# A fused two-block kernel: another order of ScalarE's work at the start, a merge kept in PSUM, two later waits, one weight chunk split on VectorE

## The chip, the cores and the metric

The kernel runs on one core of one Trainium2 chip. The metric is the device time of one execution in microseconds (us). A core has five engines that run side by side, each working through its own queue in order: TensorE (PE, matrix products), VectorE (DVE), ScalarE (ACT), GpSimd (POOL) and SyncE (SP, which here issues the DMA transfers). They wait for each other on semaphores.

## What is computed

Two residual blocks on a sequence of 256 tokens of width 1024, in float32. The first has a modulation from a conditioning vector (`ada_w`), an input projection `w_in`, a Fourier mix, a bidirectional gated scan over a context and the sequence, a merge of two branches and a convolutional feed-forward part. The second has a projection `w_in_2`, banded attention, a short convolution, a pool, `w_out_2`, and an MLP. Cut to what the change touches:

```python
# first block
hx = modulate(rmsnorm(x, norm1_g), mx[:, :, 0], mx[:, :, 1])   # sequence
hc = modulate(rmsnorm(ctx, norm1_g), mc[0], mc[1])             # context
ux = hx @ w_in;  uc = hc @ w_in
y_a = fourier_mix(ux[..., fnet]) @ w_a
y_b = y_hgrn @ w_b                                             # gated with silu(u[..., g])
merged = sigmoid(ux[..., ga]) * y_a + sigmoid(ux[..., gb]) * y_b
x = x + mx[:, :, 2] * (merged @ w_out)
# second block
out = einsum('bnhqk,bnkhd->bnqhd', softmax(scores), v)         # attention outputs
x = x + concat(y_attn, y_conv, y_pool) @ w_out_2
h2 = rms_norm(x, norm2_g)
x = x + square(relu(h2 @ w_mlp1)) @ w_mlp2
```

## The kernel before

Activations are held transposed, as tiles of 128 features by 256 tokens. Each float32 operand is split into a high part in the format `fp32r` and a low part, and every product is made of three matmuls: high weights by high activations, high by low, low by high (`mm3`, lines 1434 to 1436).

**Weights.** All weights come in chunks of 128 x 2048 (1 MB), in the order of `chunk_plan`: 20 chunks of `w_in` with 16 of `ada_hi` between them, `w_a`, `w_b` (2 each), `w_out` (4), 22 of `ffn_up` with 11 of `ffn_down`, 10 of `w_in_2`, 4 of `w_out_2`, 16 of `w_mlp1` with 16 of `w_mlp2`. SP loads a chunk into one of four `raw` buffers as soon as the low part of the chunk four places before has been made (`load`, line 400). ACT copies `raw` to `whi` (`high`, line 487; for the first seven chunks in two halves, `first_high` and `high_half`, line 490). The low part `wlo` = `raw` - `whi` is made by POOL for the chunks marked `by_pool` (line 77; lines 463 and 469, in pieces of 512 columns), and by DVE for the rest (`low`, line 864). The chunks by POOL are all those ahead of `w_mlp1`, and chunks 0 to 3 of `w_mlp1`. There are three `whi` and three `wlo` buffers. `turn` numbers the split chunks; `high(q)` makes all up to q. In the MLP's loop, DVE calls `low` for two chunks ahead, then makes relu, square and low part of the activation (lines 1394 to 1404).

**Product banks.** Products go to three PSUM banks in rotation. `product_tables` lists which semaphore says that a bank has been emptied; a group waits for the one three groups before. In `w_in` chunk 6 to 9 an instruction takes sequence and context together (512 columns). Chunks 2 and 3 are emptied by ACT to `FU`, 4 and 5 through Silu to `SG` (the semaphore `fu_sg`, `project_evict`, line 587).

**The beginning on ACT** is a queue written out by hand (lines 562 to 629). `shifts` and `scales` finish the modulation, `input_high(1, ks)` makes the high part of the context's input tiles after DVE's `input_mul` (line 926), with DVE's `input_low` (line 931) behind it. Two copies to `CP` (line 629) give DVE the row for its dot products with `ada_hi`. ACT loads a table of functions when it goes from Sqrt to Silu or Sigmoid.

**The merge.** For each of the four pieces of `w_b` (24 matmuls each) DVE multiplies the product by `GB` (line 1134), adds it to `GA` (line 1137), ACT makes the high part `MGh` (line 709), DVE the low part `MGl` (line 1139). `w_out` chunk 0 needs them in order of tiles.

**Attention outputs and column sums.** ACT writes the values `VV` after `w_in_2` 8 and 9 (line 815); TensorE makes the outputs in two halves (`tp`, lines 1854 to 1856). After `w_out_2`, TensorE sums the squares `SQ3` by columns (`square_columns`, line 1698), the first two tiles of it after DVE has added others to them (line 1164), the last two in `finish_norm`, in the middle of `w_mlp1` 0.

Of the kernel before, what the change touches and what calls it, by code (L numbers as in the profile page):

```python
# [7 lines left out]
F32 = mybir.dt.float32  # L8
F32R = mybir.dt.float32r
U8 = mybir.dt.uint8  # L10
ALU = mybir.AluOpType
ACT = mybir.ActivationFunctionType
# [58 lines left out]
def weight_tables():  # L71

    plan = chunk_plan()
    place = {(name, i): n for n, (name, i, _) in enumerate(plan)}
    split = [(name, i) for name, i, _ in plan if name != "ada_hi"]
    turn = {key: q for q, key in enumerate(split)}
    by_pool = [name not in ("w_mlp1", "w_mlp2") or name == "w_mlp1" and i < 4 for name, i in split]
    hi_at, lo_at, pool_at, dve_at = [], [], 0, 0
    for q in range(len(split)):
        hi_at.append(q + 1 + min(q + 1, FINE))  # L80
        if by_pool[q]:
            pool_at += 4 if q < FINE else 1
            lo_at.append(("lo_pool", pool_at))
        else:
            dve_at += 1
            lo_at.append(("lo_dve", dve_at))
    return plan, place, split, turn, by_pool, hi_at, lo_at


def product_tables(split):  # L90

    ends, groups, claimed, emptied = {}, 0, {}, []
    for name, i in split:
        n = {"w_a": 2, "w_b": 2}.get(name, 1)
        if name == "w_in" and 6 <= i < 12 or (name, i) in (("w_out", 3), ("w_out_2", 3)):
            n = 2
        if (name, i) in (("ffn_down", 10), ("w_mlp2", 15)):
            n = 4
        groups += n
        ends[name, i] = groups  # L100
        if name == "w_in":
            e = ([("q_done", i + 1)] if i < 2 else [("fu_sg", i - 1)] if i < 6 else
                 [("one_minus", 2 * i - 11), ("one_minus", 2 * i - 10)] if i < 10 else
                 [("v_done", 2 * i - 19), ("v_done", 2 * i - 18)] if i < 12 else
                 [("ga_done", i - 11)] if i < 16 else [("gb_done", i - 15)])
        elif name in ("w_a", "w_b"):
            e = [(f"gate_{name[2]}", 2 * i + 1), (f"gate_{name[2]}", 2 * i + 2)]
        elif name in ("w_out", "w_out_2"):
            x = "x1" if name == "w_out" else "x3"
            e = [(x, 2 * i + 2)] if i < 3 else [(x, 7), (x, 8)]  # L110
        elif name == "ffn_up":
            e = [("conv", 16 * i + 16)]
        elif name == "w_in_2":
            e = [("proj", i + 1)] if i < 8 else [("val_2", 2 * i - 14)]
        elif name == "w_mlp1":
            e = [("relu", i + 1)]
        else:
            e = []
        claimed[name, i] = len(emptied)
        emptied += e  # L120
    return ends, claimed, emptied
# [49 lines left out]
def build(nc, io):  # L171
    s = {n: nc.alloc_semaphore(n) for n in SEMS}
# [64 lines left out]
    def product(name, i, j=0):  # L237
        return bank[(claimed[name, i] + j + 1) % 3]

    def flat(ap):  # L240
        return ap.rearrange("p a b -> p (a b)")
# [230 lines left out]
    def scalar(e):  # L472
# [112 lines left out]
        def project_evict(name, i, out, func, sem):  # L585
            e.wait_ge(s["gemm"], ends[name, i])
            e.activation(out, product(name, i)[:, :], func).then_inc(s[sem], 1)

        def merge_keys(li):
            h = LEVELS[li]  # L590
            if li == 0:
                e.wait_ge(s["one_minus"], 8)
                e.wait_ge(s["diag"], 2)
            else:
                e.wait_ge(s["lev"], 2 * li)
                e.wait_ge(s["kf"], li)
            e.activation(halves(flat(KM[:, :, :]), h).rearrange("p b two z -> p two b z"), key_halves(h),
                         ACT.Copy).then_inc(s["k_merged"], 1)
# [10 lines left out]
        warm(ACT.Sqrt)  # L609
        e.wait_ge(s["sq_in"], 6)  # L610
        e.activation(RC[:, 2:4], RC[:, 2:4], ACT.Sqrt, bias=eps[:, 0:1], scale=1.0 / D).then_inc(s["rms_in"], 1)
        project_evict("w_in", 2, flat(FU[:, 0:2, :]), ACT.Copy, "fu_sg")
        first_high(5, 0)
        first_high(5, 1)
        shifts(1, 2, 14)
        shifts(1, 3, 16)
        scales(1, 0, 18)
        scales(1, 1, 20)
        input_high(1, range(0, 2))
        project_evict("w_in", 3, flat(FU[:, 2:4, :]), ACT.Copy, "fu_sg")  # L620
        input_high(1, range(2, 4))
        first_high(6, 0)
        scales(1, 2, 22)
        input_high(1, (4, 5))
        first_high(6, 1)
        scales(1, 3, 24)
        input_high(1, (6, 7))
        for n in range(2):
            e.activation(CP[:, n * 512:n * 512 + 512], CB[:, n * 512:n * 512 + 512], ACT.Copy).then_inc(s["cx_row"], 1)
        for i in range(4, 20):  # L630
            high(i + 2)
            if i == 18:
                for d in range(2):
# [4 lines left out]
            if i == 19:  # L638
                e.wait_ge(s["yf_lo"], 2)
                for hp in range(2):  # L640
# [3 lines left out]
                    e.wait_ge(s["on_done"], hp + 1)  # L644
                    e.activation(SQo[:, 2 * hp:2 * hp + 2, :], ON[:, 2 * hp:2 * hp + 2, :],
                                 ACT.Square).then_inc(s["on_sq"], 1)
            if i < 6:
                e.wait_ge(s["rms_in"], 2)
                project_evict("w_in", i, flat(SG[:, 2 * (i - 4):2 * (i - 4) + 2, :]), ACT.Silu, "fu_sg")
            elif i < 10:  # L650
                for j in range(2):
                    b = product("w_in", i, j)[:, :]
                    e.wait_ge(s["gemm"], starts["w_in", i] + j + 1)
# [51 lines left out]
        for i in range(2):  # L705
            high(turn["w_b", i] + 2)
            for n in (2 * i, 2 * i + 1):
                e.wait_ge(s["merged"], n + 1)
                e.activation(MGh[:, 2 * n:2 * n + 2, :], GA[:, 2 * n:2 * n + 2, :], ACT.Copy).then_inc(s["mg_hi"], 1)

        warm(ACT.Sqrt)
        for i in range(4):
# [144 lines left out]
    def vector(e):  # L857
# [273 lines left out]
        for n in range(4):  # L1131
            f = slice(2 * n, 2 * n + 2)
            e.wait_ge(s["gemm"], starts["w_b", 0] + n + 1)
            e.tensor_tensor(flat(GB[:, f, :]), product("w_b", n // 2, n % 2)[:, :], flat(GB[:, f, :]), ALU.mult).then_inc(s["gate_b"], 1)
            e.wait_ge(s["gate_b"], n + 1)
            e.wait_ge(s["gate_a"], n + 1)
            e.tensor_tensor(GA[:, f, :], GA[:, f, :], GB[:, f, :], ALU.add).then_inc(s["merged"], 1)  # L1137
            e.wait_ge(s["mg_hi"], n + 1)
            e.tensor_tensor(MGl[:, f, :], GA[:, f, :], MGh[:, f, :].bitcast(F32), ALU.subtract).then_inc(s["mg_lo"], 1)

        e.wait_ge(s["side"], 24)
        e.tensor_tensor(MODX[:, 0:24], MODX[:, 0:24], v("ada_b", 16, 24), ALU.add).then_inc(s["mods"], 1)
# [269 lines left out]
    def tensor(e):  # L1412
# [293 lines left out]
        bs = misc("col1")  # L1706
# [135 lines left out]
            if i == 8:  # L1842
                turn_probabilities(1)
        e.wait_ge(s["pt_done"], 6)
        e.wait_ge(s["val_2"], 4)
        for tp in range(2):
            b = misc(f"av{tp}")
            for j in range(2):
                for par in range(2):
# [17 lines left out]
        for i in range(3):  # L1867
            pair("w_out_2", i, MXh, MXl, order2, ready=mixed if i == 0 else None)
        pair("w_out_2", 3, MXh, MXl, order2, apart=True)
        e.wait_ge(s["sq3_sum"], 2)  # L1870
        square_columns(bs, SQ3, 0, 2)

        def h4_ready(k):
            e.wait_ge(s["h4_hi"], k + 1)
            e.wait_ge(s["h4_lo"], k + 1)

        def finish_norm():
            for j in range(2):
                e.wait_ge(s["sq3"], 4 + j)
                m = square_columns(bs, SQ3, 6 + j, 1)  # L1880
            m.then_inc(s["col_x"], 1)
# [139 lines left out]
```

## Time and profile before

| | us |
|---|---|
| median of 3 runs | 745.47 |
| the runs | 749.41, 745.47, 740.64 |
| the profiled execution | 743.66 |
| its span, first to last instruction | 741.8 |

All times in the rows are us from the start of this span unless marked ns. "PE" rows are matmuls, "L1434" is line 1434 of the kernel, "[... <-X]" says how long the engine was idle ahead of the instruction and what ended it. "issue" is idle time for which the profile shows no releaser. "PEclk" is the clock that TensorE was granted, as a share of full speed.

### The profile page before, as it was taken

To read this page: it belongs to the slowest core of one execution; us is meant where nothing else is said; L and a number is where in the kernel's file an instruction comes from. 1 tells how busy PE (TensorE), PEld (TensorE's weight loads), DVE (VectorE), ACT (ScalarE), POOL (GpSimd) and SP (SyncE) were. 2 spreads that over 40 slices of the span, in tenths; PEclk is the share of its full clock that TensorE was granted. 3 is DMA by queue.
4 is the path that set the end of the run, shared out by engine and by line. 5 is a ranking of instruction groups with operands and counts; after the bars stand their busy time and mean duration, and the time that the engine had idled before them with its cause. 6 is when DMAs were issued, how large, how long until landed. Compare 5 with 4: busy or idle time off the path is not lost.

```text
span 741.8 us, 14168 instructions
## 1 busy us (share of the span) xinstructions
PE 718.3 (97%) x5844; PEld 695.2 (94%) x5844; DVE 496.1 (67%) x905; ACT 360.5 (49%) x459; POOL 402.3 (54%) x223
## 2 busy tenths in 40 slices
PE   6899999999999989999999999999999899999998
PEld 3798789999999989999999999999999899999997
DVE  3877797669536569877777774558865465566663
ACT  6688134245444456555555546445554344334331
POOL 0776544556549957888878887766795400000000
PEclk9999999999999989999999999999999999999999
DMA  9994888337534537455555554433435545655611
GB/s 359 419 397 162 339 287 310 143 114 262 204 114 160 175 125 300 174 192 205 174 175 193 201 171 171 159 127 114 171 115 195 202 160 182 228 175 172 222 57 57
DMA packets 21089, 145.84 MB, mean 197 GB/s; under 512 B 2465, under 2 KB 2977, under 8 KB 3746
## 3 DMA queue, kind: packets, MB, share of 16 engines
q1 hardware_dynamic: 20880, 144.87, 53.9%
q8 instruction: 47, 0.77, 0.4%
q14 instruction: 16, 0.13, 0.0%
q10 hardware_dynamic: 146, 0.07, 0.0%
HBM read 143.88 MB, written 1.05 MB: 195 GB/s over the span
## 4 chain that ended last, share of the span: by engine, by line
PE 87%; DVE 3%; DMA 3%; ACT 3%; issue 2%; POOL 1%; DVEq 0%; ACTq 0%; POOLq 0%
PE bank L1434 23%; PE bank L1435 22%; PE bank L1436 22%; PE bank L1452 5%; DMA raw<-in_w_in 3%; PE CP L1435 2%; PE CP L1434 2%; PE CP L1436 2%; PE bank L1544 2%; ACT whi L490 1%; POOL wlo L463 1%; DVE H4l L1380 1%; PE bank L1477 1%; DVE GA L1137 1%; PE bank L1492 1%
## 5 line engine op out<-in xcount | busy, mean ns | idle before, releaser
L469 POOL TENSOR_TENSOR wlo<-raw,whi 128x512 fp32r<-128x512 f32 (+1 forms) x189 | 366.5, 1970 | 153.1 <-ACT whi L487 153.0
L487 ACT ACTIVATE whi<-raw 128x2048 fp32r<-128x2048 f32 x100 | 190.8, 1909 | 59.9 <-DMA raw<-in_w_in 32.3
L1204 DVE SCALAR_TENSOR_TENSOR Y<-bank,vec,Y 128x189 f32<-128x189 f32 (+2 forms) x352 | 123.0, 422 | 40.4 <-ACT Y L739 40.3
L1434 PE MATMUL bank<-H2h,whi 128*128 128x256 f32 x352 | 100.1, 284 | 1.7 <-DVE H2l L1179 1.7
L1435 PE MATMUL bank<-H2l,whi 128*128 128x256 f32 x352 | 100.0, 284 | 0.0
L1436 PE MATMUL bank<-H2h,wlo 128*128 128x256 f32 x352 | 99.9, 284 | 0.0
L1434 PE MATMUL bank<-H1h,whi 128*128 128x256 f32 (+1 forms) x288 | 90.0, 312 | 4.8 <-DVE H1l L931 1.9
L1436 PE MATMUL bank<-H1h,wlo 128*128 128x256 f32 (+1 forms) x288 | 88.3, 307 | 0.0
L1435 PE MATMUL bank<-H1l,whi 128*128 128x256 f32 (+1 forms) x288 | 88.2, 306 | 0.0
L864 DVE TENSOR_TENSOR wlo<-raw,whi 128x2048 fp32r<-128x2048 f32 x28 | 64.6, 2307 | 31.0 <-ACT whi L487 31.0
L1434 PE MATMUL bank<-H4h,whi 128*128 128x256 f32 x256 | 71.8, 280 | 2.4 <-ACT whi L487 2.4
L1435 PE MATMUL bank<-H4l,whi 128*128 128x256 f32 x256 | 71.3, 279 | 0.0
L1436 PE MATMUL bank<-H4h,wlo 128*128 128x256 f32 x256 | 71.3, 278 | 0.0
L1434 PEld LDWEIGHTS bank<-H2h,whi 128*128 128x128 f32 x352 | 68.7, 195 | 1.9 <-issue 1.9
L1435 PEld LDWEIGHTS bank<-H2l,whi 128*128 128x128 f32 x352 | 67.2, 191 | 0.0
L1436 PEld LDWEIGHTS bank<-H2h,wlo 128*128 128x128 f32 x352 | 67.2, 191 | 0.0
L1434 PEld LDWEIGHTS bank<-H1h,whi 128*128 128x128 f32 x288 | 55.1, 191 | 9.2 <-issue 5.5
L1435 PEld LDWEIGHTS bank<-H1l,whi 128*128 128x128 f32 x288 | 55.0, 191 | 2.8
L1436 PEld LDWEIGHTS bank<-H1h,wlo 128*128 128x128 f32 x288 | 54.8, 190 | 2.9
L1434 PE MATMUL bank<-FH,whi 128*128 128x256 f32 x192 | 53.0, 276 | 0.0
L1435 PE MATMUL bank<-FL,whi 128*128 128x256 f32 x192 | 53.0, 276 | 0.0
L1436 PE MATMUL bank<-FH,wlo 128*128 128x256 f32 x192 | 53.0, 276 | 0.0
(327 smaller groups left out, 1899.9 us busy)
## 6 DMA issues: line engine op xcount, KB each, us to landing
raw<-in_w_mlp SPq DMA_DIRECT2D x32, 1024.0 KB, 4.9
raw<-in_w_in SPq DMA_DIRECT2D x30, 1024.0 KB, 6.5
raw<-in_ffn_up SPq DMA_DIRECT2D x22, 1024.0 KB, 4.9
raw<-in_ada_hi SPq DMA_DIRECT2D x16, 1024.0 KB, 5.5
raw<-in_ffn_down SPq DMA_DIRECT2D x11, 1024.0 KB, 4.8
raw<-in_w_out SPq DMA_DIRECT2D x8, 1024.0 KB, 4.9
ada_s<-in_ada_s SPq DMA_DIRECT2D x4, 1024.0 KB, 17.9
ada_p<-in_ada_p SPq DMA_DIRECT2D x2, 1024.0 KB, 10.1
```

What stands on the lines that cost most here:

```text
L463: e.tensor_tensor(part(l, kp, 1), part(r, kp, 1), part(h, kp, 1).bitcast(F32), ALU.subtract).then_inc(s["lo_pool"], 1)
L469: m = e.tensor_tensor(l[:, a:a + step], r[:, a:a + step], h[:, a:a + step].bitcast(F32), ALU.subtract)
L487: e.activation(whi[q % NHI][:, :], raw[n % NRAW][:, :], ACT.Copy).then_inc(s["w_hi"], 1)
L490: e.activation(part(whi[q % NHI], 2 * half, 2), part(raw[place[split[q]] % NRAW], 2 * half, 2), ACT.Copy).then_inc(s["w_hi"], 1)
L864: e.tensor_tensor(l[:, :], r[:, :], h[:, :].bitcast(F32), ALU.subtract).then_inc(s["lo_dve"], 1)
L1137: e.tensor_tensor(GA[:, f, :], GA[:, f, :], GB[:, f, :], ALU.add).then_inc(s["merged"], 1)
L1204: e.scalar_tensor_tensor(o[:, r0:r1, c0:c1], z[:, r0 + dr:r1 + dr, c0 + dc:c1 + dc], cw[:, f, tap:tap + 1], o[:, r0:r1, c0:c1], ALU.mult, ...
L1434: e.matmul(out, h[:, col:col + P], xh, start=first, stop=False, skip_group_check=True)
L1435: e.matmul(out, h[:, col:col + P], xl, start=False, stop=False, skip_group_check=True)
L1436: return e.matmul(out, l[:, col:col + P], xh, start=False, stop=last, skip_group_check=True)
L1452: m = e.matmul(out, x, w, start=k + t + n == 0, stop=(k, n) == (KT - 1, 2), skip_group_check=True)
L1544: m = e.matmul(b[:, hd * P:(hd + 1) * P], KM[:, hd, t * P:(t + 1) * P], q, start=True, stop=True)
```

## The change

Six edits. (1) ACT's queue at the start gets another order: the halves of chunk 5, the evictions of chunks 2 and 3, and the context's input tiles are interleaved differently. (2) The Silu evictions of chunks 4 and 5 (`output_gate`) leave the loop and stand earlier, and the high part of chunk 7 stands ahead of the `CP` copies; the wait for `rms_in` ahead of the evictions is dropped. (3) The merge works in place in the product bank: product and sum are written to PSUM, high and low part read from there; the bank is free only after the low part. (4) Each half of the attention outputs waits for its own values. (5) The first column sums move from ahead of `w_mlp1` 0 into `finish_norm`. (6) `w_mlp1` chunk 3 has its low part made by DVE.

```diff
-    by_pool = [name not in ("w_mlp1", "w_mlp2") or name == "w_mlp1" and i < 4 for name, i in split]
+    by_pool = [name not in ("w_mlp1", "w_mlp2") or name == "w_mlp1" and i < 3 for name, i in split]
...
         elif name in ("w_a", "w_b"):
-            e = [(f"gate_{name[2]}", 2 * i + 1), (f"gate_{name[2]}", 2 * i + 2)]
+            freed = "gate_a" if name == "w_a" else "mg_lo"
+            e = [(freed, 2 * i + 1), (freed, 2 * i + 2)]
...
+        def output_gate(i):
+            project_evict("w_in", i, flat(SG[:, 2 * (i - 4):2 * (i - 4) + 2, :]), ACT.Silu, "fu_sg")
+
...
         e.activation(RC[:, 2:4], RC[:, 2:4], ACT.Sqrt, bias=eps[:, 0:1], scale=1.0 / D).then_inc(s["rms_in"], 1)
-        project_evict("w_in", 2, flat(FU[:, 0:2, :]), ACT.Copy, "fu_sg")
-        first_high(5, 0)
-        first_high(5, 1)
         shifts(1, 2, 14)
         shifts(1, 3, 16)
         scales(1, 0, 18)
         scales(1, 1, 20)
+        first_high(5, 0)
         input_high(1, range(0, 2))
+        project_evict("w_in", 2, flat(FU[:, 0:2, :]), ACT.Copy, "fu_sg")
+        input_high(1, range(2, 4))
+        first_high(5, 1)
+        scales(1, 2, 22)
         project_evict("w_in", 3, flat(FU[:, 2:4, :]), ACT.Copy, "fu_sg")
-        input_high(1, range(2, 4))
         first_high(6, 0)
-        scales(1, 2, 22)
         input_high(1, (4, 5))
         first_high(6, 1)
+        output_gate(4)
         scales(1, 3, 24)
         input_high(1, (6, 7))
+        high(7)
         for n in range(2):
             e.activation(CP[:, n * 512:n * 512 + 512], CB[:, n * 512:n * 512 + 512], ACT.Copy).then_inc(s["cx_row"], 1)
-        for i in range(4, 20):
+        output_gate(5)
+        for i in range(6, 20):
             high(i + 2)
...
-            if i < 6:
-                e.wait_ge(s["rms_in"], 2)
-                project_evict("w_in", i, flat(SG[:, 2 * (i - 4):2 * (i - 4) + 2, :]), ACT.Silu, "fu_sg")
-            elif i < 10:
+            if i < 10:
...
-                e.activation(MGh[:, 2 * n:2 * n + 2, :], GA[:, 2 * n:2 * n + 2, :], ACT.Copy).then_inc(s["mg_hi"], 1)
+                e.activation(flat(MGh[:, 2 * n:2 * n + 2, :]), product("w_b", i, n % 2)[:, :], ACT.Copy).then_inc(s["mg_hi"], 1)
...
-            e.tensor_tensor(flat(GB[:, f, :]), product("w_b", n // 2, n % 2)[:, :], flat(GB[:, f, :]), ALU.mult).then_inc(s["gate_b"], 1)
+            b = product("w_b", n // 2, n % 2)[:, :]
+            e.tensor_tensor(b, b, flat(GB[:, f, :]), ALU.mult).then_inc(s["gate_b"], 1)
             e.wait_ge(s["gate_b"], n + 1)
             e.wait_ge(s["gate_a"], n + 1)
-            e.tensor_tensor(GA[:, f, :], GA[:, f, :], GB[:, f, :], ALU.add).then_inc(s["merged"], 1)
+            e.tensor_tensor(b, b, flat(GA[:, f, :]), ALU.add).then_inc(s["merged"], 1)
             e.wait_ge(s["mg_hi"], n + 1)
-            e.tensor_tensor(MGl[:, f, :], GA[:, f, :], MGh[:, f, :].bitcast(F32), ALU.subtract).then_inc(s["mg_lo"], 1)
+            e.tensor_tensor(flat(MGl[:, f, :]), b, flat(MGh[:, f, :]).bitcast(F32), ALU.subtract).then_inc(s["mg_lo"], 1)
...
         e.wait_ge(s["pt_done"], 6)
-        e.wait_ge(s["val_2"], 4)
         for tp in range(2):
+            e.wait_ge(s["val_2"], 2 * tp + 2)
...
-        e.wait_ge(s["sq3_sum"], 2)
-        square_columns(bs, SQ3, 0, 2)
...
         def finish_norm():
+            e.wait_ge(s["sq3_sum"], 2)
+            square_columns(bs, SQ3, 0, 2)
```

## Rows read from the trace of the kernel before

**Rows 1.** The page, part 1: busy time, share of the span, instructions.

```profile
PE 718.3 (97%) x5844; PEld 695.2 (94%) x5844; DVE 496.1 (67%) x905; ACT 360.5 (49%) x459; POOL 402.3 (54%) x223
```

**Rows 2.** Waits of TensorE: who for whom; us in total, times, longest.

```profile
PE bank L1434 <- ACT whi L487: 2.4, 1, 2.4
...
PE bank L1434 <- issue: 1.8, 2, 1.1
PE bank L1434 <- DVE H2l L1179: 1.7, 1, 1.7
PE bank L1434 <- DVE MGl L1139: 1.3, 1, 1.3
PE bank L1698 <- DVE SQ L1164: 1.1, 1, 1.1
PE CP L1854 <- issue: 1.0, 1, 1.0
...
PE bank L1434 <- ACT SG L587: 0.5, 1, 0.5
```

**Rows 3.** Stretches: length, busy PE, PEld, DVE, ACT, POOL (instructions), PEclk, DMA share, GB/s.

```profile
264.80:269.70 4.90, 4.90 (x23) 4.90 (x24) 4.72 (x13) 3.29 (x7) 0.00 (x0) 0.50 0.51 199
557.00:581.70 24.70, 24.23 (x212) 24.18 (x212) 13.66 (x17) 11.30 (x13) 15.26 (x11) 1.00 0.48 168
...
584.30:587.70 3.40, 3.40 (x18) 3.40 (x19) 1.99 (x1) 0.00 (x0) 0.00 (x0) 0.57 0.73 251
```

**Rows 4.** Timeline of TensorE around its two waits in w_in 6 and 7.

```profile
67.37 0.39 PE L1436 MATMUL bank<-H1h,wlo 128*128 128x512 f32 x1
68.29 0.50 PE L1434 MATMUL bank<-H1h,whi 128*128 128x512 f32 x1 [0.52 <-ACT SG L587]
...
73.75 0.39 PE L1436 MATMUL bank<-H1h,wlo 128*128 128x512 f32 x1
75.25 0.47 PE L1434 MATMUL bank<-H1h,whi 128*128 128x512 f32 x1 [1.10 <-issue]
```

**Rows 5.** Timeline of ACT, 51 to 70 us: start, us, instruction, count.

```profile
51.39 2.00 ACT L490 ACTIVATE whi<-raw 128x1024 fp32r<-128x1024 f32 x2
...
57.65 0.47 ACT L553 ACTIVATE H1h<-bank,MOD 128x256 fp32r<-128x256 f32 x1 [0.43 <-DVE bank L926]
...
66.34 1.28 ACT L587 ACT_TABLE_LOAD   x1
67.64 0.60 ACT L587 ACTIVATE SG<-bank 128x512 f32<-128x512 f32 x1
68.13 1.91 ACT L487 ACTIVATE whi<-raw 128x2048 fp32r<-128x2048 f32 x1
```

**Rows 6.** Timeline of POOL: the last pieces of w_in 5; w_in 7 and 8.

```profile
55.88 2.55 POOL L463 TENSOR_TENSOR wlo<-raw,whi 128x512 fp32r<-128x512 f32 x2
...
70.12 10.03 POOL L469 TENSOR_TENSOR wlo<-raw,whi 128x512 fp32r<-128x512 f32 x8 [5.59 <-ACT whi L487]
```

**Rows 7.** Instructions on tile GA: ns min/median/max, first and last start.

```profile
L1108 DVE TENSOR_TENSOR GA<-bank,GA x4: 680/687/693, 215.2 to 225.1; 128x512 f32<-128x512 f32 x4
L1137 DVE TENSOR_TENSOR GA<-GA,GB x4: 693/1068/1073, 228.6 to 238.5; 128x512 f32<-128x512 f32 x4
L709 ACT ACTIVATE MGh<-GA x4: 632/633/635, 229.4 to 239.6; 128x512 fp32r<-128x512 f32 x4
L1139 DVE TENSOR_TENSOR MGl<-GA,MGh x4: 989/1004/1007, 230.0 to 240.2; 128x512 fp32r<-128x512 f32 x4
```

**Rows 8.** Timeline of ACT: the second pair of values.

```profile
530.37 0.84 ACT L815 ACTIVATE VV<-bank,RC 128x256 f32<-128x256 f32 x2 [2.86 <-PE bank L1452]
```

**Rows 9.** Timeline of DVE: the low part of w_mlp2 0, first of its chunks.

```profile
569.97 2.29 DVE L864 TENSOR_TENSOR wlo<-raw,whi 128x2048 fp32r<-128x2048 f32 x1 [0.80 <-ACT whi L487]
```

**Rows 10.** Timeline of ACT: the high part of w_mlp1 3.

```profile
574.16 1.90 ACT L487 ACTIVATE whi<-raw 128x2048 fp32r<-128x2048 f32 x1
```

**Rows 11.** Timeline of POOL: the low part of w_mlp1 3, in four pieces.

```profile
576.15 8.00 POOL L469 TENSOR_TENSOR wlo<-raw,whi 128x512 fp32r<-128x512 f32 x4 [7.53 <-ACT whi L487]
```

## The prediction

> **What bounds the kernel now.** The page comes first: TensorE is busy 97% of the span, the other engines at most 67% [rows 1]. So time can only come out of what TensorE does not do, and the list of its waits says what that is [rows 2]. Seven rows matter. The change has something to say to six of them: the wait for `whi` L487 (2.4 us), one of the two "issue" waits at a bank (1.1 us), `MGl` (1.3 us), `SQ` L1164 (1.1 us), the "issue" wait at L1854 (1.0 us), and `SG` (0.5 us). The seventh, `H2l` (1.7 us), it leaves alone. The table of stretches then shows that a wait can cost more than itself [rows 3]: from 557 to 581.7 us the granted clock is 1.00 (2.4 GHz) and TensorE starts 212 matmuls in 24.23 us, 0.114 us each. In the 3.4 us behind the 2.4 us wait the granted clock is 0.57, nearly all of it at 1.2 GHz, and behind the `H2l` wait it is 0.50 for 4.9 us. A stretch loses its length times what is missing of the clock: 3.4 x 0.43 = 1.5 us behind the first. The 1.1 us wait for `SQ`, at the start of the clean stretch from 557 us, is followed by none.
>
> **The beginning (two parts: ACT's order and the hoisted gates).** TensorE stands at 67.37 to 68.29 and at 73.75 to 75.25 us [rows 4]. A 512-column matmul starts every 0.23 us there, so the losses are 0.92 - 0.23 = 0.7 and 1.50 - 0.23 = 1.3 us. The first is the bank of w_in 4, which `SG` L587 empties. ACT comes to it only at 67.64, behind a table load of 1.28 us at 66.34 [rows 5], though w_in 4 was multiplied 11 us earlier (48 matmuls of w_in 5 at 0.114 and 24 of 512 columns at 0.23 lie between). The second is the low half of w_in 7: ACT makes its high half at 68.13 (1.91 us), GpSimd subtracts from 70.12 in pieces of 10.03/8 = 1.25 us [rows 6], four of them end at 75.1, and TensorE starts at 75.25. The new order puts `output_gate(4)` ahead of the last two `scales`, and `high(7)` ahead of the two `CP` copies and of `output_gate(5)`. I walked ACT's new queue with its own durations. The gate needs only 1.28 + 0.60 us at about 61.3, ending at 63.2, well before 67.4. ACT was idle there in part, waiting for DVE's dots, so the 1.9 us is mostly paid from idle time. Then `high(7)` starts at about 65 in place of 68.1, its low half is done at about 72, and TensorE wants it at 67.6 + 24 x 0.23 = 73.2. Both waits go: **2.0 us**.
>
> What is moved pays for it. The halves of w_in 5 stood at 51.39 (2.00 us for both). The first now stands behind four `shifts` and four `scales`, and comes about 1.4 us later. The second also stands behind an eviction and `input_high` of tiles 0 to 3, which wait for DVE (0.43 us before the last of them) [rows 5]. I get about 56.6 to 57.6 for it. GpSimd's last piece of w_in 5 then ends at about 57.7 + 2 x 1.25 = 60.2 instead of 55.88 + 2.55 = 58.4 [rows 6]. TensorE asks for it at 60.7: it ends w_in 6's first group at 67.6, so w_in 5 starts at 67.6 - 24 x 0.23 - 48 x 0.114 = 56.6, and the last quarter comes after 36 matmuls. It fits with some 0.4 us to spare; that is the tightest place, and each tenth above it is lost once. The first `FU` eviction moves from just ahead of 51.39 to about 54.5; its bank is wanted at 56.6. The `CP` copies come 1.5 us later, and with them DVE's first dots, whose raw buffers feed the later loads on SP's queue. But that queue also waits for the low half of w_in 7 (75.1, now 72), so the loads come earlier, not later. Both ends for this part: 0 (w_in 5 loses what w_in 7 gains) and 2.0; I take 2.0, since every term is a measured duration.
>
> **Merging in PSUM.** Per piece DVE and ACT do in series: product, sum, high part, low part. Before: 0.69 + 1.07 + 0.63 + 1.00 = 3.4 us [rows 7], and TensorE makes a piece in 24 x 0.114 = 2.7 us. The lag grows by 0.7 per piece, and at the end w_out 0 waits 1.3 us [rows 2]. The sum and the low part read two SBUF tensors, and the sum took 0.69 once and 1.07 in most cases; a product with one operand in PSUM took 0.68 to 0.69 in all four [rows 7]. With a PSUM operand in all three I price them at 0.69: 3 x 0.69 + 0.63 = 2.7 us, the pace of TensorE. The fourth piece is then ready 2.7 us after its product, and TensorE has 36 matmuls, 4.1 us, before it asks. The whole wait goes: **1.3 us**. Banks are now held until `mg_lo`: w_b's last piece needs the first piece's bank 5.4 us after its product, it is free after 2.7. Bounds: 1.3, and, if all three operations take 1.07 in PSUM, a loss: pieces of 3.8 us, 0.4 more than now, and the wait longer by 4 x 0.45 = 1.8. I take 1.3, as the product is the nearest row. The Trainium skill (VectorE: DVE Perf Modes, "The TRN2 errata" and "Rules for kernel authors") speaks against this part: it gives VectorE 58 fixed cycles for an SBUF source and 120 for a PSUM source, and advises a copy to SBUF first when many operations follow. By its figures the sum and the low part would each cost some 0.06 us more than now, an estimate from that page, and this part would lose about 0.5 us instead of gaining. The trace does not agree: 0.687 us with a PSUM source against 0.693 at best without.
>
> **Attention outputs.** TensorE waits 1.0 us at L1854 [rows 2]: it asks for all four values, and the last two are ACT's `VV` pair at 530.37, 0.84 us, which itself starts only when TensorE has finished w_in_2 9 [rows 8]. The first half of the outputs needs only the earlier pair. It now starts at once and covers the second pair (1.5 us of matmuls against 0.9): **1.0 us**. The bound below is 0, if DVE's low part of the first output came late. It doesn't, as w_out_2 begins with the pooled tiles.
>
> **Column sums.** TensorE waits 1.1 us for DVE's `SQ` sum before w_mlp1 0 [rows 2]. Moved behind 30 matmuls of w_mlp1 0 (3.4 us), the wait has long been met. The sums themselves cost the same there. The reciprocal root behind them has about 0.2 us of slack by my walk of ACT's queue, so 0.9 to 1.1: **1.1 us**.
>
> **Fourth w_mlp1 chunk.** GpSimd takes 8.00 us for its four pieces from 576.15 [rows 11], right behind the high half at 574.16 + 1.90 [rows 10], and TensorE waits for the end, 584.15. (The list names ACT; GpSimd is what came last.) DVE needs 2.29 us for such a chunk [rows 9]: ready at about 578.4, 3.3 us before TensorE asks (581.7). DVE's queue behind it is `relu(2)`, square and low part, about 2 us later than now. Nobody asks for these before contraction 2, two chunks later. The low part of w_mlp2 1 comes behind them on DVE, done near 582.5, and is asked for at 581.7 + 48 x 0.114 = 587.2. So the 2.4 us go, and with them the 1.5 us of slow clock that followed: **3.9 us**. Bounds: 2.4 if the slow stretch turns up elsewhere, 3.9 if not.
>
> **The sum.** 2.0 + 1.3 + 1.0 + 1.1 + 3.9 = 9.3 us. Nothing later gives it back. TensorE has no wait between 75 and 239 us, so its partners keep ahead, and their loads hang on the same events and move with it. The profiled run took 743.66 us (span 741.8), so it would be 734.4. The median of the three runs is 1.8 us above that, so on its scale 745.47 - 9.3 = **736.2 us**.
>
> **Rivals.**
> - *The slow stretch stays* (TensorE is granted 1.2 GHz somewhere else after the start, as it is at 264.8): 736.2 + 1.5 = 737.7, or up to 738.6 with a stretch of 4.9 us instead. For it: the waits near 262 to 265 us remain. Chance 0.17.
> - *The beginning gives nothing*: the late second half of w_in 5 or a late `high(7)` makes a new wait, 738.2. Against: 0.4 us of slack by rows; for: six things in one queue, each with a small wait. Chance 0.15.
> - *PSUM operands are slow for DVE* : all three at 1.07, so the `MGl` wait stays and grows by 1.8: 736.2 + 3.1 = 739.3. Against: the product's 0.687. Chance 0.03. (The page's cycle counts, named above, point the same way.)
> - *The change does little*: TensorE, earlier by 2 to 5 us, meets the raw buffers' loads or GpSimd where both now just keep up, and most waits reappear behind others; 741 to 746. GpSimd is busy 54%, with no wait of TensorE for it between 76 and 580. Chance 0.12.
> - *Slower*: one place could do it, `first_high(5, 1)` standing behind `input_high` of tiles 2 and 3 on ACT. It waits for DVE, and GpSimd, w_in 6 and w_in 7 stand behind it. Each us beyond the 0.4 is paid once, and beyond a wait of about 2 us comes 1.5 us of slow clock. To undo the 7.3 us of the other parts and pass the old time by 1% it would have to be some 13 us late, where the row shows 0.43: 753 us. Chance 0.03.
>
> The forecast itself has 0.50. A measurement of this kernel can tell about 1% from no change (the three runs lie from 740.64 to 749.41), so "faster" is below 738.0: nearly all of the forecast's cases, and half of the first two rivals: 0.60. Within 1%: 0.37. Slower: 0.03. The range takes the slow stretch behind `H2l` shrinking (another 1 to 2 us) and the spread of runs below, 731.5, and the rivals above, 741.5.
>
> **What would show it.** In the profile after: no wait for `SG` and no "issue" wait near 74 us; TensorE starts w_in 7 near 73.2; `merged` adds at 0.69 us and GpSimd's pieces beside them at 1.25; no `MGl`, `SQ` L1164 and L1854 waits; `wlo` of w_mlp1 3 on DVE near 570; granted clock 1.00 from about 270 us to the end. I am wrong if TensorE waits for `wlo` L463 near 60 us, if the sums in PSUM take 1 us, or if a new stretch at 0.5 stands where none was.

## The result, and the profile after

| | before | changed |
|---|---|---|
| median, us (4 runs each) | 747.44 | 730.07 |
| lowest to highest | 740.64 to 749.56 | 728.25 to 734.75 |
| profiled execution | 743.66 | 730.14 |
| its span | 741.8 | 728.3 |

The ratio is 0.9859 (95% interval 0.9816 to 0.9901): faster, though by less than 2%. The ratios and intervals, here and below, leave out slow executions (over 1.5% above the fastest of the same kernel), so they are not the ratios of the medians or means beside them; the means are over all executions, and without the slow ones the difference of the two means that follow would be 8.8 us. The median lies 1.4 us below the low end of the range. Four runs turned out to be few. In the experiments below the old kernel ran 87 times with mean 742.5 us, and the changed one, its four runs above included, 22 times with mean 733.8. The difference of these means is 8.7 us (standard error 0.9), and 8.0 without those four runs; the forecast was 9.3.

**TensorE's waits.** From the list for the changed kernel: who waits for whom, us in total, times, longest. Its helper lines stand five below the old ones (L1439 to L1441 are the three matmuls of `mm3`).

```profile
...
PE bank L1439 <- ACT H1h L554: 2.1, 1, 2.1
PE bank L1439 <- DVE H1l L935: 1.9, 1, 1.9
PE bank L1439 <- DVE H2l L1184: 1.7, 1, 1.7
PE bank L1439 <- POOL wlo L470: 1.5, 1, 1.5
PE bank L1439 <- issue: 1.0, 1, 1.0
...
```

Against [rows 2], the rows for `whi` L487, `MGl`, `SQ`, L1854 (now L1859) and `SG` are gone, and so is the old 1.1 us "issue" wait of w_in 7. `H2l` is as it was. Another "issue" wait (1.0 us) is new. The wait for `wlo` L470 (1.5 us) is an old one grown: in the old profile it is the other part, 0.65 us, of the "issue" row. The `H1h` wait stands at 33 us, ahead of the change; it is 0.5 or 2.0 to 2.1 us in profiles of either kernel.

**The merge.** Instructions on the tiles `GA` and `MGh`, `MGl` of the changed kernel, ns as min/median/max, then first and last start; the product, from the timeline of DVE, is the last row.

```profile
L1142 DVE TENSOR_TENSOR bank<-bank,GA x4: 699/700/700, 228.4 to 236.5; 128x512 f32<-128x512 f32 x4
L713 ACT ACTIVATE MGh<-bank x4: 597/599/600, 229.2 to 237.3; 128x512 fp32r<-128x512 f32 x4
L1144 DVE TENSOR_TENSOR MGl<-bank,MGh x4: 691/692/692, 229.8 to 237.9; 128x512 fp32r<-128x512 f32 x4
...
230.41 0.69 DVE L1139 TENSOR_TENSOR bank<-bank,GB 128x512 f32<-128x512 f32 x1
```

The sum fell from 1.07 to 0.70 us and the low part from 1.00 to 0.69 [rows 7]. Four pieces start 2.7 us apart (228.4 to 236.5), which is TensorE's own pace.

**Outputs and the last chunk.** First TensorE's first output and ACT's second pair of values, then DVE's low part of w_mlp1 3, all from timelines of the changed kernel.

```profile
522.19 0.43 PE L1859 MATMUL CP<-PT,VV 128*64 128x128 f32 x2
522.29 0.84 ACT L819 ACTIVATE VV<-bank,RC 128x256 f32<-128x256 f32 x2 [2.87 <-PE bank L1457]
...
567.32 2.29 DVE L868 TENSOR_TENSOR wlo<-raw,whi 128x2048 fp32r<-128x2048 f32 x1 [1.12 <-ACT whi L488]
```

The outputs start before the second pair does. The low part of w_mlp1 3 is ready at 569.6 instead of 584.15 [rows 11], and nobody waits for it.

**The clock.** Stretches of the changed kernel: window, its length, busy us and instructions of PE, PEld, DVE, ACT, POOL, then PEclk, DMA share, GB/s.

```profile
261.20:268.00 6.80, 5.75 (x27) 5.78 (x28) 5.93 (x15) 4.85 (x9) 0.00 (x0) 0.50 0.39 151
268.00:443.00 175.00, 174.97 (x1543) 174.80 (x1543) 136.58 (x401) 99.73 (x123) 144.73 (x33) 1.00 0.55 197
551.00:580.00 29.00, 29.00 (x258) 29.00 (x257) 18.83 (x20) 12.98 (x14) 6.90 (x5) 1.00 0.52 183
580.00:724.00 144.00, 144.00 (x1273) 144.00 (x1272) 85.06 (x68) 54.16 (x37) 0.00 (x0) 1.00 0.47 164
```

The stretch at 0.57 behind w_mlp1 3 [rows 3] is gone and none has taken its place. The one near the `H2l` wait stays.

**Where the 13.5 us between the two profiled executions lie.** I compared the start of the same matmul in both, at the borders of the stages (rounded; 13.6 us at the last one):

| stretch | gain, us | what it is |
|---|---|---|
| to w_out 0 (235.8) | 0.2 | the beginning, net |
| to the end of w_out | 2.3 | `MGl` wait 1.4, the rest a quicker rhythm |
| feed-forward | 6.3 | no wait, a quicker rhythm |
| start of w_in_2 | -0.8 | wait of 1.5 where there was 0.65 |
| to the outputs | 1.2 | outputs 1.0 |
| w_out_2 | -0.8 | a slower rhythm |
| to w_mlp1 0's rows | 1.2 | column sums |
| to the end | 4.1 | w_mlp1 3: wait 2.4, slow clock |

The waits that the change removes thus gave about 8 us. The other 5.6 us, net of the two losses, came from something that the prediction doesn't have at all: above all, TensorE ran the same matmuls of the feed-forward part faster.

### The profile page after: what moved, and what is told of

The parts are those of the page before. It is cut to its first block, busy times and chain, and to the rows that moved or that the text cites. A ratio compares the mean times of both kernels' runs of the same rounds, so it can differ in the third digit from the quotient of the medians.

```text
span 728.3 us, 14164 instructions
## 1 busy us (share of the span) xinstructions
PE 708.5 (97%) x5844; PEld 685.5 (94%) x5844; DVE 491.5 (67%) x906; ACT 360.1 (49%) x459; POOL 390.0 (54%) x219
## 4 chain that ended last, share of the span: by engine, by line
PE 90%; DMA 4%; DVE 2%; SPq 2%; ACT 1%; issue 1%; POOL 1%; DVEq 0%; ACTq 0%
PE bank L1439 24%; PE bank L1441 24%; PE bank L1440 24%; PE bank L1457 5%; DMA TOK<-in_ctx_tok 4%; PE bank L1549 2%; PE CP L1441 1%; PE CP L1439 1%; PE CP L1440 1%; DVE Y L1209 1%; SPq L413 1%; POOL wlo L470 1%; SPq L410 1%; PE bank L1805 1%; PE bank L1464 0%
## 5 line engine op out<-in xcount | busy, mean ns | idle before, releaser
L470 POOL TENSOR_TENSOR wlo<-raw,whi 128x512 fp32r<-128x512 f32 (+1 forms) x185 | 354.2, 1945 | 138.3 <-ACT whi L488 138.2
L1439 PE MATMUL bank<-H2h,whi 128*128 128x256 f32 x352 | 98.6, 280 | 1.8 <-DVE H2l L1184 1.7
L1440 PE MATMUL bank<-H2l,whi 128*128 128x256 f32 x352 | 98.4, 280 | 0.0
L1441 PE MATMUL bank<-H2h,wlo 128*128 128x256 f32 x352 | 98.3, 279 | 0.0
L1439 PE MATMUL bank<-H1h,whi 128*128 128x256 f32 (+1 forms) x288 | 89.2, 310 | 5.5 <-ACT H1h L554 2.1
L868 DVE TENSOR_TENSOR wlo<-raw,whi 128x2048 fp32r<-128x2048 f32 x29 | 66.4, 2292 | 31.6 <-ACT whi L488 31.6
L1441 PE MATMUL bank<-H1h,wlo 128*128 128x256 f32 (+1 forms) x288 | 87.4, 304 | 0.0
L1439 PE MATMUL bank<-H4h,whi 128*128 128x256 f32 x256 | 70.9, 277 | 0.0
L1441 PE MATMUL bank<-H4h,wlo 128*128 128x256 f32 x256 | 70.7, 276 | 0.0
L1439 PEld LDWEIGHTS bank<-H2h,whi 128*128 128x128 f32 x352 | 67.4, 191 | 2.1 <-issue 2.1
L1441 PEld LDWEIGHTS bank<-H2h,wlo 128*128 128x128 f32 x352 | 67.3, 191 | 0.0
L1439 PEld LDWEIGHTS bank<-H1h,whi 128*128 128x128 f32 x288 | 54.2, 188 | 9.7 <-issue 6.5
L1441 PEld LDWEIGHTS bank<-H1h,wlo 128*128 128x128 f32 x288 | 54.2, 188 | 2.9
L1439 PE MATMUL bank<-FH,whi 128*128 128x256 f32 x192 | 53.0, 276 | 0.0
L1441 PE MATMUL bank<-FH,wlo 128*128 128x256 f32 x192 | 53.0, 276 | 0.0
```

What stands on the lines that cost most here:

```text
L470: m = e.tensor_tensor(l[:, a:a + step], r[:, a:a + step], h[:, a:a + step].bitcast(F32), ALU.subtract)
L868: e.tensor_tensor(l[:, :], r[:, :], h[:, :].bitcast(F32), ALU.subtract).then_inc(s["lo_dve"], 1)
L1439: e.matmul(out, h[:, col:col + P], xh, start=first, stop=False, skip_group_check=True)
L1440: e.matmul(out, h[:, col:col + P], xl, start=False, stop=False, skip_group_check=True)
L1441: return e.matmul(out, l[:, col:col + P], xh, start=False, stop=last, skip_group_check=True)
```

## The rhythm of the feed-forward part

The windows are cut where TensorE has no wait and the granted clock is 1.00. First the old kernel, two of its profiled executions (the second is the run `base_again` below).

```profile
280.00:300.00 20.00, 20.00 (x172) 20.00 (x172) 20.00 (x60) 12.30 (x16) 14.43 (x4) 1.00 0.65 245
400.00:420.00 20.00, 20.00 (x172) 20.00 (x172) 15.32 (x47) 9.98 (x14) 16.33 (x4) 1.00 0.60 202
640.00:660.00 20.00, 20.00 (x179) 20.00 (x178) 12.15 (x10) 8.18 (x6) 0.00 (x0) 1.00 0.61 211
```

```profile
280.00:300.00 20.00, 20.00 (x179) 20.00 (x178) 20.00 (x60) 12.21 (x18) 15.36 (x4) 1.00 0.67 258
400.00:420.00 20.00, 20.00 (x172) 20.00 (x172) 15.31 (x47) 9.98 (x14) 16.58 (x4) 1.00 0.59 204
```

Then the changed kernel, also two executions, the one above and the run `after_again`.

```profile
280.00:300.00 20.00, 20.00 (x179) 20.00 (x178) 20.00 (x61) 12.05 (x18) 15.30 (x4) 1.00 0.62 231
400.00:420.00 20.00, 20.00 (x179) 20.00 (x178) 15.96 (x49) 11.62 (x14) 17.22 (x4) 1.00 0.57 206
```

```profile
280.00:300.00 20.00, 20.00 (x179) 20.00 (x178) 20.00 (x60) 11.71 (x17) 15.29 (x4) 1.00 0.63 240
400.00:420.00 20.00, 20.00 (x172) 20.00 (x171) 15.32 (x46) 11.22 (x14) 15.08 (x5) 1.00 0.53 182
```

There are two levels only in such windows of all fourteen profiles: 178 or 179 matmuls, and 172 or 173. Averaged over their starts, the 256-column matmuls begin every 113.3 ns in the one and every 117.8 ns in the other. In the feed-forward part a rhythm holds over hundreds of matmuls and changes at a pause, if at all. From 305 to 312 us there is a pause of 0.2 us in the profiles that were in the quick rhythm by then. Behind it seven of these twelve went on slow and five quick, to about 450 us, `after_again` and `after_third` (the same kernel) among them on different sides. The same 1480 matmuls (from the 1901st on) took 168.0 us in the five, 173.2 in the seven and 174.3 in the two that were slow throughout.

The single times fall in steps of that size: the changed kernel's 22 lie in groups at 728 to 730 (6), 733 to 735.5 (12) and 738.6 to 740.4 (4), with nothing between; the old kernel's 87 stand nearly the same step apart, 32 of them from 737.3, 46 from 742 and 9 from 748.5 us up. One stretch with two rhythms explains one such step; no profile of either kernel falls in the topmost group, so what makes that one stays open. Four runs of each drew three from the changed kernel's lowest group, and from 740.6, 745.5 and two of about 749.5 for the old one. Compared group by group, which takes this luck out, the changed kernel lies 9.7, 9.4 and 10.3 us below the old one.

I didn't find what draws the rhythm. For the feed-forward part it is drawn per execution: the changed kernel has both there, the old one has both from 280 to 300 us, and the groups get much the same share of either kernel's executions (37, 53 and 10% of the old one's, 27, 55 and 18% of the changed one's). In two shorter stretches it goes with the change. `w_out` runs slow in four of the five profiles with the old merge, and only behind the waits that the new merge takes away; it is quick in all nine with the new merge. The matmuls of `w_out_2` right behind the attention outputs are slow in all nine profiles with edit 4, and in one of the five without it.

## The experiments

**The old kernel again**, for its spread.

> The kernel before, unchanged, once more. Its first profile has matmuls of 256 columns starting every 117.8 ns from 242 to 457 us (w_out 1 to the end of ffn_up and ffn_down) and every 113.3 ns after 587 us; the changed kernel has 113.3 ns from 268 to 452 us too. Theory 1 (chance): which of the two rhythms a stretch gets is drawn anew in each execution, so this profile has another pattern of the two, and if the feed-forward stretch comes out at 113.3 ns the profiled time is about 7 us lower (736 to 738) with the same waits. Theory 2 (the program decides): the same pattern as in the first profile, 117.8 ns from 242 to 457 us, time 742 to 745 us. The ratio is 1.00 by both.

Mean of its ten 742.8, ratio 1.0001 (0.9955 to 1.0047). Its profile, of 744.97 us, is quick from 280 to 300 us and slow behind that, so the pattern is drawn anew, but the long stretch came out slow again. It has the waits of [rows 2] to 0.2 us, and the slow clock behind the wait of w_mlp1 3. It also has a stretch at half clock behind the `SQ` wait at 558.0, and a wait of 0.77 us at the first matmul of `w_out` (236.57 us), which the first profile did not have.

**One part alone.** `chunk_only` is the old kernel with edit 6 only:

```diff
-    ... or name == "w_mlp1" and i < 4 for name, i in split]
+    ... or name == "w_mlp1" and i < 3 for name, i in split]
```

> Only w_mlp1 3's low part on DVE. Theory of the waits: the 2.4 us wait ahead of w_mlp1 3 and the slow clock of 1.5 us behind it go, 3.9 us less than before. Rival: the slow stretch comes elsewhere, 2.4 us less. Whatever more or less the time shows is the rhythm of TensorE in other stretches: 7 us less if the feed-forward stretch runs at 113.3 ns in place of 117.8.

`merge_only` has edit 3 only: the merge in the bank, with `mg_lo` as what frees it.

> Only the merge in PSUM. Theory of the waits: the 1.3 us wait ahead of w_out 0 goes, 1.4 us less. Rival, the rhythm follows from that wait: without it w_out and the feed-forward stretch behind it keep the rhythm of w_b, 113.3 ns, and the kernel is 8 to 9 us faster by this edit alone.

`begin_only` has edits 1 and 2, ACT's order.

> Only the new order of ACT in the beginning. By my step of the prediction 2.0 us less. By the trace of the changed kernel: ACT stands 1.5 us at the first context tile because DVE waits for TensorE's row (L1445 there), the second half of w_in 5 comes 2 us later than I had it, TensorE waits 1.0 us in w_in 5, and by w_in 10 nearly nothing is left: 0.2 to 0.9 us less.

`waits_only` has edits 4 and 5, outputs and column sums.

> Only the two weaker waits of the second block (attention outputs, column sums). By my sum 1.0 + 1.1 = 2.1 us less than before. In two of three profiles of kernels that have it (the kernel before once more, and the one with the beginning alone) the wait for the column sums is followed by a stretch of 3.4 us at clock 0.50 from 558 us; if it is the wait that brings it, it is gone here, worth another 1.7 us in those executions.

| kernel | ratio (95%) | mean less the old kernel's 742.5, us | forecast |
|---|---|---|---|
| chunk_only | 0.9969 (0.9937 to 1.0002) | -3.2 (s.e. 0.8) | -3.9 |
| merge_only | 0.9975 (0.9938 to 1.0011) | -3.3 (1.1) | -1.4 |
| begin_only | 0.9991 (0.9954 to 1.0028) | -1.5 (1.0) | -2.0; by the trace, -0.2 to -0.9 |
| waits_only | 0.9966 (0.9933 to 0.9999) | -1.8 (1.5) | -2.1 |

The four add up to 9.8 (s.e. about 2.5), the whole gives 8.7: no part takes from another beyond the error. By its interval only `waits_only` is clear of no change, and barely. A single time can't size a part of 1 to 2 us, since the rhythm alone moves an execution by 5. The profiles can, by the time from one matmul to another some hundreds further on in each of the fourteen.

- *Merge.* In `merge_only` the `MGl` row is gone, and the low part took 0.692 us. It shows more: the wait at `w_out`'s first matmul (0.77 us in four of the five profiles with the old merge, in none of the nine with the new one) and the slow rhythm of `w_out` are gone too. The 300 matmuls from the 1501st on took 36.3 to 37.2 us with the old merge and 34.0 in all nine with the new one: 2.3 to 3.2 us, as the mean of `merge_only` says and not the 1.4 forecast. So its rival held for `w_out`; behind the `H2l` wait, in the feed-forward part, it did not (quick in four of nine with the new merge, one of five with the old one).
- *Outputs and column sums.* In `waits_only` the `SQ` and L1854 rows are gone. The 400 matmuls from the 4001st on took 45.9 to 47.5 us without these edits and 44.5 with them: 1.4 to 3.1 us.
- *Chunk.* In `chunk_only` `whi` L487's long wait is gone. The 250 matmuls from the 4401st on took 31.7 to 34.5 us with GpSimd on w_mlp1 3 and 28.3 in all seven without: 3.4 to 6.2 us.
- *Beginning.* In `begin_only` the old waits are gone and the new one is there, before any other edit could have made it:

```profile
60.88 0.36 PE L1437 MATMUL bank<-H1h,whi 128*128 128x256 f32 x1 [0.98 <-issue]
```

**The whole again, and the whole without edit 6.** `after_again` and `after_third` are the changed kernel. `all_but_chunk` and `chunk_back_2` are one kernel, the changed one with `i < 4` put back.

> The changed kernel once more. Theory of the waits: seen over many executions the change is worth the waits it removes and the slow clock behind them: 0.5 (beginning) + 1.4 (merge) + 1.0 (outputs) + 1.2 (columns) + 3.9 (chunk) = 8.0 us, ratio 0.989. Rival, the rhythm belongs to the change: as in its first profile, the feed-forward stretch runs at 113.3 ns in every execution where before it mostly runs at 117.8, worth up to 6 us more: ratio 0.981.

> The changed kernel with w_mlp1 3's low part back on GpSimd. TensorE waits about 2.4 us for it (573 to 575 us) and a stretch of 3.4 us at clock 0.50 follows, as before: 3.9 us slower than the changed kernel. Rival: the slow stretch in the first profile of before was chance, it is absent here, and only the 2.4 us show.

> The changed kernel a third time, as the yardstick for the three beside it. The executions so far lie in groups some 5 us apart (before near 738, 743 and 749 us; changed near 729, 734 and 739), as if the feed-forward stretch of about 140 us ran at one of two rhythms, 113.3 or 117.8 ns per matmul, in each execution. Theory: the groups stay where they are, shifted against before by 9 us, and only how many fall in each differs: ratio 0.985 to 0.991. Rival: the groups belong to chips or days, and the changed kernel always has the faster one: ratio 0.981.

> The changed kernel with w_mlp1 3 back on GpSimd, again with more rounds: its first measurement was only 0.8 to 1.1 us above the changed kernel where its profile has 3.1 us of wait and a slow stretch of 6.8 us (3.4 us lost). Theory: the wait and the slow clock are real and cost 3.1 us + 1.7 to 3.4 us, and the first measurement had more executions of the faster rhythm; now 3 to 5 us above. Rival: the wait is really worth only 1 us, since a later wait is shortened by it.

The changed kernel had 0.9897 (0.9862 to 0.9931) and 0.9873 (0.9819 to 0.9927), as both theories had it; both rivals said 0.981, that the quick rhythm belongs to the change. With the chunk back it had 0.9912 (0.9880 to 0.9944) and 0.9914 (0.9875 to 0.9952). Over 22 executions of each, the means are 733.8 and 736.8: edit 6 gives 3.0 us (s.e. 1.1) here too, at the low end of the 3 to 5 expected. `chunk_back_2` shows the place: TensorE's first matmul of w_mlp1 3, GpSimd's four pieces, and three stretches.

```profile
578.03 0.36 PE L1439 MATMUL bank<-H4h,whi 128*128 128x256 f32 x1 [3.08 <-issue]
569.95 7.98 POOL L470 TENSOR_TENSOR wlo<-raw,whi 128x512 fp32r<-128x512 f32 x4 [7.52 <-ACT whi L488]
...
551.00:574.90 23.90, 23.90 (x210) 23.76 (x209) 14.23 (x17) 11.30 (x13) 14.45 (x11) 1.00 0.47 171
578.70:582.10 3.40, 3.40 (x19) 3.40 (x18) 1.38 (x1) 0.00 (x0) 0.00 (x0) 0.50 0.89 323
582.10:600.00 17.90, 17.90 (x159) 17.90 (x159) 8.74 (x8) 6.63 (x5) 0.00 (x0) 1.00 0.61 233
```

The wait is 3.1 us now, more than the old 2.4, since the rows ahead of it come earlier. Behind it 3.4 us are granted 0.50, which costs 1.7 us. That does not always follow. `waits_only` has the same wait and no slow clock behind it:

```profile
577.19 0.36 PE L1434 MATMUL bank<-H4h,whi 128*128 128x256 f32 x1 [3.11 <-issue]
...
577.20:581.00 3.80, 3.80 (x33) 3.80 (x34) 2.04 (x1) 0.00 (x0) 0.00 (x0) 1.00 0.75 261
```

Of the seven profiles with this wait, six have a slow stretch behind it (five of 3.4 us, one of 6.8). So edit 6 takes away a wait of 2.3 to 3.1 us in each of the seven, and 1.7 us more (once 3.4) in six.

**Two repairs.** `half_early` is the changed kernel with one line moved, so that the second half of w_in 5 no longer stands behind DVE's work:

```diff
         first_high(5, 0)
+        first_high(5, 1)
         input_high(1, range(0, 2))
         project_evict("w_in", 2, ...)
         input_high(1, range(2, 4))
-        first_high(5, 1)
```

> The changed kernel with both halves of w_in 5 ahead of the first context tile, alone. In the profile of both edits together TensorE has no wait near 60 us and starts w_in 10's transposes near 118 us in place of 120.2 to 121. So 1.0 to 1.5 us less than the changed kernel, and the wait of 0.7 to 1.5 us ahead of w_in_2 0 stays.

0.9828 (0.9780 to 0.9875), mean of six 730.1, which is 3.7 us (s.e. 1.2) below the changed kernel, more than the 1.0 to 1.5 expected; the start of a matmul, counted below, gives 1.5. Its profile (a slow-rhythm one, 731.5 us) has no wait of TensorE between 50 and 78 us. `half_table` and `half_table_2` are one kernel: that edit, and ACT's load of the Sqrt table put behind the high part of w_in_2 0.

```diff
-            if i == 22:
-                warm(ACT.Sqrt)
             if i >= 5 and i % 2:
                 high(turn["ffn_down", (i - 5) // 2] + 2)
+            if i == 23:
+                warm(ACT.Sqrt)
```

> The changed kernel with two edits: both halves of w_in 5 stand together ahead of the context's first input tile, where ACT waits 1.5 us for DVE, and the table load for Sqrt at the end of ffn_up stands behind the high part of w_in_2 0, for whose low part TensorE waits 1.5 us at 446 us. If the second half of w_in 5 is what TensorE waits for near 60 us, that wait of 1.0 us goes; if the high part of w_in_2 0 is what GpSimd lacks, 1.3 of the 1.5 us go. Together 2.3 us less than the changed kernel. Rival: GpSimd is busy anyway in both places and hands the wait on, 0 to 0.5 us.

> Both edits again, with more executions (6 the first time). By the waits 1.0 to 1.5 us from the beginning and 0.7 to 1.3 us from the table load, 2 to 3 us less than the changed kernel: ratio to before 0.986 to 0.987.

0.9865 (0.9804 to 0.9927) and 0.9820 (0.9761 to 0.9878); mean of the twelve 731.2, 2.6 us below the changed kernel. All 18 executions with the line moved have mean 730.9, 2.9 us (s.e. 1.2) below the changed kernel. I can't tell the table's part from nothing by these times (731.2 against 730.1). The profile shows its wait gone.

## Why the prediction was right, and where it was not

**Right in sign and in most of its terms.** The `MGl` wait (forecast 1.3, found 1.4), the outputs (1.0, 1.0), the column sums (1.1, 1.2) and the chunk (3.9, 4.1 between the profiles, 3.0 and 3.2 between means) came as worked out. Neither the table of cycles in the Trainium skill (VectorE: DVE Perf Modes, "The TRN2 errata") nor its advice to copy to SBUF first held here: sum and low part out of PSUM took 0.700 and 0.692 us, against 0.693 at best out of SBUF, a difference of 0.01 us and not of 0.06.

What made the old ones slow was GpSimd beside them. The old kernel has the same comparison elsewhere: the low part of the activation (L1404) reads two SBUF tensors too, and took 0.69 us while GpSimd was idle and 1.02 during GpSimd's work of [rows 11].

```profile
574.29 0.69 DVE L1404 TENSOR_TENSOR FL<-FQ,FH 128x512 fp32r<-128x512 f32 x1 [0.70 <-ACT FH L853]
...
578.69 1.02 DVE L1404 TENSOR_TENSOR FL<-FQ,FH 128x512 fp32r<-128x512 f32 x1 [0.70 <-ACT FH L853]
```

GpSimd loses as well: its pieces took 1.72 to 1.77 us beside the old merge and 1.30 to 1.32 beside the new one (I had written 1.25). Which of the two is held up varies: the old sum at 228.63 us took 0.693 with GpSimd at work, and the same one 1.64 in `base_again`. Another page of the Trainium skill says that a DVE instruction with two SBUF inputs contends with a GpSimd instruction that reads SBUF (SBUF — State Buffer, "Who interferes with whom"); the trace agrees, 1.07 against 0.70.

**The merge was priced too low.** The prediction counts one row, the `MGl` wait of a profile in which `w_out`'s first matmul did not wait, and it has no rhythm. The wait of 0.77 us there in the other four profiles with the old merge, and the slow rhythm of `w_out` behind it, bring this term from 1.3 to 2.3 to 3.2 us. The profile names ACT's `whi` as what ends the 0.77 us; in `base_again` that copy was done 0.6 us before the matmul and GpSimd's piece 0.2 us before it, so the stretched pieces of GpSimd are the likelier cause. That is argued, not tested. The sum came out near partly by luck: the merge gave at least 1.0 us more than forecast and the beginning 1.5 less.

**The beginning failed: 2.0 us forecast, 0.2 to 0.5 found** (the mean of `begin_only`, 1.5 with s.e. 1.0, can't tell them apart). Both old waits went, as forecast, though their work comes 2 us later than I walked it: the gate runs at 64.75 (forecast: done by 63.2) and `high(7)` starts at 67.10 (forecast: about 65). But the step "the second half of w_in 5 at 56.6 to 57.6, it fits with some 0.4 us to spare" was wrong. ACT, DVE, ACT, POOL and PE of the changed kernel, from timelines:

```profile
53.27 1.04 ACT L491 ACTIVATE whi<-raw 128x1024 fp32r<-128x1024 f32 x1
55.26 0.88 DVE L930 SCALAR_TENSOR_TENSOR bank<-CX,A,bank 128x256 f32<-128x256 f32 x2 [2.70 <-PE bank L1445]
55.84 0.87 ACT L554 ACTIVATE H1h<-bank,MOD 128x256 fp32r<-128x256 f32 x2 [1.53 <-DVE bank L930]
...
58.74 1.05 ACT L491 ACTIVATE whi<-raw 128x1024 fp32r<-128x1024 f32 x1
59.87 7.53 POOL L464 TENSOR_TENSOR wlo<-raw,whi 128x512 fp32r<-128x512 f32 x6 [2.94 <-ACT whi L491]
61.24 0.36 PE L1439 MATMUL bank<-H1h,whi 128*128 128x256 f32 x1 [0.98 <-issue]
```

I let `shifts` and `scales` start DVE's first context tile as soon as they were done, at 53.3. DVE also needs the row that TensorE spreads over the partitions (L1445), and that came at 55.2. TensorE has its own time for it, whatever ACT does (54.4 in the old profile, in which the matmuls up to there also stand 0.7 to 1.0 us earlier). In the old order that row and ACT's scales came together: the same DVE instruction stood at 54.54, released by `A`, so the trace of before named only the scale. So ACT reached the first tile early, stood 1.53 us at it with the second half of w_in 5 behind it, and made that half at 58.74. GpSimd's first piece of it ended at 61.1, and TensorE waited 0.98 us. That is the rival "the beginning gives nothing", for its own reason. `half_early` turns it round: ACT makes both halves in what would be idle time, and the wait of 1.5 us shrinks to 0.3.

```profile
52.85 2.00 ACT L491 ACTIVATE whi<-raw 128x1024 fp32r<-128x1024 f32 x2
55.14 0.87 ACT L554 ACTIVATE H1h<-bank,MOD 128x256 fp32r<-128x256 f32 x2 [0.29 <-DVE bank L930]
```

The start of TensorE's 1501st matmul (of 5844, near 223 us) sizes it across all profiles, rhythm and clock of later stages left out: 223.6 on average in the five with the old order, 223.1 in the six with the new one, 221.5 in the three with `half_early`'s. The new order is worth 0.5 us, and with one line moved 2.1, about what I had forecast for the order without it.

**"Nothing later gives it back" held for the change, but not for a quick rhythm.** After the feed-forward part TensorE asks for w_in_2 0 at its own pace, but ACT loads the Sqrt table first, and GpSimd starts 1.4 us later for it. ACT, POOL and PE of the changed kernel:

```profile
438.02 1.28 ACT L503 ACT_TABLE_LOAD   x1
439.31 0.20 ACT L503 ACTIVATE warmed<-eps 128x1 f32<-128x1 f32 x1
439.42 3.71 ACT L488 ACTIVATE whi<-raw 128x2048 fp32r<-128x2048 f32 x2
441.40 8.79 POOL L470 TENSOR_TENSOR wlo<-raw,whi 128x512 fp32r<-128x512 f32 x7 [3.84 <-ACT whi L488]
446.53 0.36 PE L1439 MATMUL bank<-H3h,whi 128*128 128x256 f32 x1 [1.50 <-POOL wlo L470]
```

The same wait is 0.65 us in the old profile and in `after_again`, which had the slow rhythm, and 1.5 in those with the quick one, `merge_only` and `waits_only` too. So it is not the change that feeds it but the rhythm: a quicker TensorE gives 0.8 us of it back here. In `half_table` it is gone:

```profile
435.22 1.91 ACT L488 ACTIVATE whi<-raw 128x2048 fp32r<-128x2048 f32 x1
437.14 1.28 ACT L503 ACT_TABLE_LOAD   x1
...
442.37 0.36 PE L1439 MATMUL bank<-H3h,whi 128*128 128x256 f32 x1
```

**The range was too narrow for four runs.** It took the spread of three runs as noise around one time. The executions fall in groups 5 us apart, and 6 of the 22 of the changed kernel lie below 731.5. The sum itself (forecast 9.3; about 8 us by the waits of the first two profiles, 8.7 by means, 9.4 to 10.3 group by group) was nearer than the median of four suggests.

## What to carry to other kernels

When an instruction is moved up in a hand-written queue, write down everything that each instruction now ahead of it waits for, producers on other engines included; one that was never the last to arrive in the old trace becomes so in the new order. Put work whose inputs are there ahead of the first instruction that waits. And before a few us are read out of single times, count matmuls in an undisturbed window of several profiles of each kernel: where the counts differ between executions of one kernel, that difference isn't the change; where they differ only between the kernels, it may be.

## What was not expected of the hardware

- At a granted clock of 1.00 and with no wait, 256-column matmuls with their weight loads start every 113.3 or every 117.8 ns. In the feed-forward part a rhythm lasts 140 us or more and may change at a pause as short as 0.2 us; it moves this kernel by 5 us of 740, and the engines beside TensorE have nearly the same busy time in both. In `w_out` the slow one came only behind a wait, and went with it.
- A DVE and a GpSimd instruction side by side that each read two SBUF tensors mostly lengthen each other: 1.00 to 1.07 us in place of 0.69, and 1.72 to 1.77 in place of 1.30. With one DVE operand in PSUM neither is lengthened.
- A wait of 2.3 to 3.1 us was followed by half clock in six of seven profiles, for 3.4 or 6.8 us. The 1.1 us wait for `SQ`, of which I wrote that no slow stretch follows it, was followed by one of 3.4 us in three of the four profiles that have it (`merge_only`: 18 matmuls in the 3.4 us from 549.7); in `chunk_only` the wait is 0.5 us and no slow stretch follows. So later column sums may have brought more than their wait; the first profile of before, on which I rested, was the exception.
